# Second modulation part read from idle split buffers and partly run in the Fourier part, heads fed in pairs to the output projection

## What is computed

```python
mod_l = (silu(c) @ w_ada + b_ada).reshape(b, 6, 1, d)      # sh1, sc1, gt1, sh2, sc2, gt2
hl = rms_norm(xl, g_mix_norm) * (1 + sc1) + sh1
q, k, v, f = split(hl @ w_in)                               # k, v also for 256 context rows
attn = per head h (4), query block (2): a = softmax(q0 k0) - lam * softmax(q1 k1); o = a @ v
o = rms_norm(o, g_subln) * (1 - lambda_init)                # per head, 128 wide
fr = real(fft2(f per group)); four = fr @ w_fourier         # 4 groups of 128
xl = xl + gt1 * (concat([o, four]) @ w_out)
h2l = rms_norm(xl, g_ffn_norm) * (1 + sc2) + sh2
xl = xl + gt2 * hier_moe(h2l)                               # 32 experts, 2 a token
```

## Time and profile before

| what | us |
|---|---|
| median of 3 runs (1869.19, 1869.19, 1871.25) | 1869.19 |
| the profiled execution, its own time | 1870.13 |
| its span, first to last instruction | 1868.4 |
| PE busy in the span | 1804.5 (97%) |
| PEld (weight loads) | 1434.0 (77%) |
| DVE / ACT / POOL | 900.1 / 723.5 / 169.5 |
| mean granted clock of TensorE | 0.982 of full |

### The profile page before, as it was taken

The page is one execution under the profiler, slowest core; times in us unless marked ns, Lnnn a source line. Parts: engine busy times, 40 slices in busy tenths (PEclk is TensorE's granted clock), DMA queues, the critical chain, the costliest instruction groups (busy, mean ns, idle before and its releaser), DMA issues.

```text
span 1868.4 us, 27467 instructions
## 1 busy us (share of the span) xinstructions
PE 1804.5 (97%) x11302; PEld 1434.0 (77%) x11302; DVE 900.1 (48%) x1108; ACT 723.5 (39%) x913; POOL 169.5 (9%) x83
## 2 busy tenths in 40 slices
PE   6997899999999998999999999999999999999998
PEld 4983845545455447999987889998999899999997
DVE  4315611111111108655676575667666756566554
ACT  3424311111111116444434554455445555354443
POOL 0100000000000000111000111111111001112110
PEclk8999899999999999999899999999999999999999
DMA  9329699999999994655534265555555554455550
GB/s 336 120 91 343 228 390 422 421 422 422 422 422 422 422 406 154 208 180 185 186 129 155 69 203 181 183 199 190 188 186 192 202 181 165 159 174 182 186 195 24
DMA packets 192158, 445.65 MB, mean 239 GB/s; under 512 B 9189, under 2 KB 140638, under 8 KB 164166
## 3 DMA queue, kind: packets, MB, share of 16 engines
q1 hardware_dynamic: 188736, 437.84, 63.6%
q10 hardware_dynamic: 2918, 4.46, 0.7%
q0 software_dynamic: 416, 2.10, 0.3%
HBM read 443.31 MB, written 1.06 MB: 238 GB/s over the span
## 4 chain that ended last, share of the span: by engine, by line
PE 90%; DVE 5%; ACT 2%; DMA 1%; issue 1%; POOL 0%; ACTq 0%; DVEq 0%
PE wk L748 16%; PE wk L1158 12%; PE wk L750 8%; PE acc L720 6%; PE acc L721 6%; PE acc L722 6%; PE wk L1178 6%; PE wk L1120 3%; PE wk L720 3%; PE wk L722 3%; PE wk L721 3%; PE acc L1136 3%; PE wk L799 2%; PE wk L800 2%; PE wk L802 1%; DVE w_lo L550 1%
## 5 line engine op out<-in xcount | busy, mean ns | idle before, releaser
L550 DVE TENSOR_TENSOR w_lo<-ring,w_hi 128x2048 fp32r<-128x2048 f32 x197 | 450.5, 2289 | 237.1 <-ACT w_hi L541 236.5
L748 PE MATMUL wk<-h_both,w_hi 128*128 128x512 f32 x1344 | 476.5, 398 | 2.2 <-DVE gated L2347 1.9
L541 ACT ACTIVATE w_hi<-ring 128x2048 fp32r<-128x2048 f32 x198 | 377.4, 1907 | 244.1 <-PE acc L722 127.2
L750 PE MATMUL wk<-h_both,w_lo 128*128 128x256 f32 x1344 | 377.3, 281 | 0.0
L748 PEld LDWEIGHTS wk<-h_both,w_hi 128*128 128x128 f32 x1344 | 252.6, 188 | 64.0 <-DVE w_lo L550 2.6
L720 PE MATMUL acc<-hid_hi,w_hi 128*128 128x256 f32 x896 | 254.4, 284 | 1.4 <-DVE arena L2556 0.8
L750 PEld LDWEIGHTS wk<-h_both,w_lo 128*128 128x128 f32 x1344 | 253.9, 189 | 0.0
L721 PE MATMUL acc<-hid_lo,w_hi 128*128 128x256 f32 x896 | 253.5, 283 | 0.0
L722 PE MATMUL acc<-hid_hi,w_lo 128*128 128x256 f32 x896 | 253.4, 283 | 0.0
L1952 POOL TENSOR_TENSOR hid_lo<-gated,hid_hi 128x512 fp32r<-128x512 f32 x44 | 124.3, 2826 | 1150.7 <-ACT hid_hi L1773 1150.7
L720 PEld LDWEIGHTS acc<-hid_hi,w_hi 128*128 128x128 f32 x896 | 171.6, 191 | 4.0 <-DVE arena L2556 1.0
(11 more groups left out here) (381 smaller groups left out, 2452.7 us busy)
## 6 DMA issues: line engine op xcount, KB each, us to landing
ring<-in_ffn_w_in_dram SPq DMA_DIRECT2D x88, 1024.0 KB, 5.1
ring<-in_w_gate_dram SPq DMA_DIRECT2D x64, 1024.0 KB, 13.7
ex_ring<-in_w_up_dram SPq DMA_DIRECT2D x64, 1024.0 KB, 16.9
ring<-in_ffn_w_out_dram SPq DMA_DIRECT2D x44, 1024.0 KB, 4.9
ex_ring<-in_w_down_dram SPq DMA_DIRECT2D x32, 1024.0 KB, 13.6
arena<-in_w_down_dram SPq DMA_DIRECT2D x32, 1024.0 KB, 12.6
ring<-in_w_ada_dram SPq DMA_DIRECT2D x24, 1024.0 KB, 7.0
ring<-in_b_w_in_dram SPq DMA_DIRECT2D x24, 1024.0 KB, 5.1
```

The source lines that it names most:

```text
L541: nc.scalar.activation(w_hi[:, v % SPLIT, 0:n], ring[:, u % RING, 0:n], ACT.Copy).then_inc(w_hi_ready, 1)
L550: eng.tensor_tensor(w_lo[:, v % SPLIT, 0:n], ring[:, u % RING, 0:n], w_hi[:, v % SPLIT, 0:n].bitcast(F32), ALU.subtract).then_inc(w_lo_rea ...
L748: mm(banks[:, m, :], wh[:, k, f], h_both[:, k, :, :], start=k == 0, stop=False, skip_group_check=True)
L750: last = mm(banks[:, m, T:2 * T], wl[:, k, f], h_hi[:, k, :], start=False, stop=k == KT - 1, skip_group_check=True)
```

## The change

The eight units 4 to 9, 14 and 15 of the second modulation part no longer go through the ring. They are loaded in pairs into the idle split buffers: `ada_pair(a, q)` loads units a and a + 1 into `w_hi` and `w_lo` of buffer q. The pairs (4, 5), (6, 7), (8, 9) are issued when the input units 13, 14 and 15 have been used; (14, 15) when unit 9 has been used. The other eight keep the ring (`ADA_RING`); `place` and `prior` give the ring slot and the unit that held it before. Their semaphores are those of the expert ring, so the counts that the experts wait for are raised (`ada_landings`).

TensorE runs the first eight units amid the Fourier part, two after each of: two groups of `over_tokens`, the other two, `over_channels`, `own_matrix`. The first `mod_row` and `ada_cols` come at the head of attention. In the loop, steps 0 and 1 have two units, steps 2 to 5 one, steps 6 and 7 none; `mod_row(2)` comes in step 5 of ScalarE and `ada_cols(2)` in step 6 of TensorE. The output projection's first split comes in step 4 (high part) and step 6 (low part, between `combine(6)` and `combine(7)`), the second's high part in step 6. The heads' norm gives its high and low part by pairs of heads (`heads_scaled`, `heads_low`), and the output projection takes the pairs (k = 0, 1), then (k = 2, 3), as they come; only the last quarter of each of its first three units closes the unit.

```diff
+ADA_RING = (0, 1, 2, 3, 10, 11, 12, 13)
+def place(u):
+    if u < U_ADA2 + 4:
+        return u
+    return u - 6 if u < U_OUT else u - 8
+def prior(u):
+    p = place(u) - RING
+    return p if p < U_ADA2 + 4 else p + 6 if p < U_ADA2 + 8 else p + 8
...
         ex_in = [sem(f"ex_in{j}") for j in range(EX_RING)]
+        ada_in = [ex_in[RING + q] for q in range(SPLIT)]
+        ada_landings = {RING: 32, RING + 1: 64, RING + 2: 32}
         ex_done, pick_ready = sem("ex_done"), sem("pick_ready")
...
-            n = 16 * (u // RING + 1)
-            eng.wait_ge(weights_in[u % RING], n if i is None else i * (16 * TURN // RING) + n)
+            n = 16 * (place(u) // RING + 1)
+            eng.wait_ge(weights_in[place(u) % RING], n if i is None else i * (16 * TURN // RING) + n)
         TAIL = split_of(U_A + 2)
+        AFTER_ADA = {split_of(U_OUT): U_ADA2 + 6, split_of(U_OUT + 1): U_ADA2 + 8, split_of(U_OUT + 2): U_ADA2 + 16}
...
             if v >= SPLIT:
-                d = unit_of(v - SPLIT) + 1
+                d = AFTER_ADA.get(v, unit_of(v - SPLIT) + 1)
                 nc.scalar.wait_ge(unit_done, d if i is None else i * TURN + d)
...
-                p = u - RING
-                if p < 0:
+                if place(u) < RING:
                     return
+                p = prior(u)
                 v = split_of(p)
...
                 vacant(u, i)
-                sp.dma_start(dst, src).then_inc(weights_in[u % RING], 16)
+                sp.dma_start(dst, src).then_inc(weights_in[place(u) % RING], 16)
...
                 fetch(U_IN + a, slot_cols(U_IN + a), in_v[a])
-            for a in range(16):
-                fetch(U_ADA2 + a, ring[:, (U_ADA2 + a) % RING, :], ada_v[1 + a // KT, a % KT])
+            def ada_fetch(a):
+                fetch(U_ADA2 + a, ring[:, place(U_ADA2 + a) % RING, :], ada_v[1 + a // KT, a % KT])
+            def ada_pair(a, q):
+                for j in range(2):
+                    sp.dma_start(ex_ring[:, q + SPLIT * j, :], ada_v[1 + (a + j) // KT, (a + j) % KT]).then_inc(ada_in[q], 16)
+            for a in range(4):
+                ada_fetch(a)
+            for v in range(5, 8):
+                sp.wait_ge(unit_done, unit_of(v) + 1)
+                ada_pair(4 + 2 * (v - 5), v % SPLIT)
+            for a in range(10, 14):
+                ada_fetch(a)
+            sp.wait_ge(unit_done, U_ADA2 + 10)
+            ada_pair(14, 7 % SPLIT)
             for a in range(4):
...
-                arrived(u)
+                a = u - U_ADA2
+                if a < 0 or a in ADA_RING:
+                    arrived(u)
+                    w = ring[:, place(u) % RING, :]
+                else:
+                    q = 7 % SPLIT if a >= 14 else (5 + (a - 4) // 2) % SPLIT
+                    pe.wait_ge(ada_in[q], 64 if a >= 14 else 32)
+                    w = ex_ring[:, q + SPLIT * (a % 2), :]
                 for gr in range(ADA_GROUPS):
                     last = mm(accf[32 * gr:32 * gr + 32, bank * 512:(bank + 1) * 512], csil[:, k, :],
-                              ring[:, u % RING, gr * 512:(gr + 1) * 512], start=(k == 0), stop=(k == KT - 1),
+                              w[:, gr * 512:(gr + 1) * 512], start=(k == 0), stop=(k == KT - 1),
                               skip_group_check=True)
...
+            def ada_second(*units):
+                for a in units:
+                    ada_rows(U_ADA2 + a, a % KT, 1)
             pe.wait_ge(grp_out, 12)
-            for gr in range(4):
+            for gr in range(2):
                 group(lambda b: over_tokens(b, gr))
+            pe.wait_ge(rope_done, 2)
+            ada_second(0, 1)
+            for gr in range(2, 4):
+                group(lambda b: over_tokens(b, gr))
+            ada_second(2, 3)
             pe.wait_ge(grp_out, 16)
...
                 group(lambda b: over_channels(b, pair))
+            ada_second(4, 5)
             pe.wait_ge(grp_out, 18)
...
                 group(lambda b: own_matrix(b, pair))
+            ada_second(6, 7)
...
             scores(0)
+            scores(1)
+            ada_cols(1)
             for s in range(8):
-                if s + 1 < 8:
+                if 0 < s < 7:
                     scores(s + 1)
-                if s == 4:
-                    ada_cols(1)
-                for a in (2 * s, 2 * s + 1):
-                    ada_rows(U_ADA2 + a, a % KT, 1)
+                ada_second(*((8, 9), (10, 11), (12,), (13,), (14,), (15,), (), ())[s])
+                if s == 6:
+                    ada_cols(2)
                 turn(s)
...
                     head_squares(0)
-            ada_cols(2)
             values(3)
...
+            def mixed(a, ks, closes=False):
+                return project3(accf[:, a * 512:(a + 1) * 512], part[a], ks=ks, opens=ks[0] == 4, closes=closes)
+            part = [split(U_OUT)]
+            mixed(0, (4, 5))
+            head_squares(1)
+            project3(accf[:, 0:512], part[0], ks=(6, 7), opens=False, closes=False)
+            part.append(split(U_OUT + 1))
+            mixed(1, range(4, 8))
+            pe.wait_ge(mix_lo_ready, 2)
+            mixed(0, (0, 1))
+            mixed(1, (0, 1))
             pe.wait_ge(mod_ready, 2)
-            part = []
+            part.append(split(U_OUT + 2))
+            mixed(2, range(4, 8))
+            mixed(2, (0, 1))
+            pe.wait_ge(mix_lo_ready, 3)
             for a in range(3):
-                part.append(split(U_OUT + a))
-                project3(accf[:, a * 512:(a + 1) * 512], part[a], ks=range(4, 8), closes=False)
-                if a == 0:
-                    head_squares(1)
-            pe.wait_ge(mix_lo_ready, 2)
-            for a in range(3):
-                project3(accf[:, a * 512:(a + 1) * 512], part[a], ks=range(4), opens=False).then_inc(unit_done, 1)
+                mixed(a, (2, 3), closes=True).then_inc(unit_done, 1)
             pe.wait_ge(rt_side, 1)
...
                     for j in range(2):
-                        pe.wait_ge(ex_in[2 * s + j], at(16 * (p + 1), 16))
+                        pe.wait_ge(ex_in[2 * s + j], at(ada_landings.get(2 * s + j, 0) + 16 * (p + 1), 16))
...
             a_values(HEADS2 - 1)
-            pe.wait_ge(mix_lo_ready, 2 + HEADS2)
+            pe.wait_ge(mix_lo_ready, 3 + HEADS2)
             for a in range(4):
...
+            mod_row(1, U_ADA2 + 8, 1)
             exps(0)
...
                     exps(s + 1)
-                if s % 4 == 3:
-                    mod_row(1 + s // 4, U_ADA2 + 2 * s + 2, 1)
-                if s == 7:
-                    split_high(9)
                 turned(s)
-                if s == 6:
-                    split_high(8)
+                if s == 5:
+                    mod_row(2, U_ADA2 + 16, 1)
                 if s % 2 == 1 and s >= 3:
                     head_out(s // 2 - 1)
-                if s == 5:
+                if s == 4:
+                    split_high(8)
+                elif s == 5:
                     head_square(0)
+                elif s == 6:
+                    split_high(9)
             act.wait_ge(reldist_out, 16)
...
             head_root(1)
-            act.wait_ge(sub_done, 1)
-            A(h_hi[:, 0:4, :], mixT[:, 0:4, :], ACT.Copy).then_inc(mix_hi_ready, 1)
+            for j in range(2):
+                act.wait_ge(sub_done, j + 1)
+                A(h_hi[:, 2 * j:2 * j + 2, :], mixT[:, 2 * j:2 * j + 2, :], ACT.Copy).then_inc(mix_hi_ready, 1)
             split_high(11)
...
                 combine(s)
-            split_low(8)
-            dve.wait_ge(modcol_ps, 3)
-            modulation(16, 48)
-            V.scalar_tensor_tensor(a_ffn, mod[:, 32:40, 0], 1.0, g_ffn, ALU.add, ALU.mult).then_inc(mod_ready, 1)
+                if s == 6:
+                    split_low(8)
             split_low(9)
-            for j in range(2):
+            def heads_scaled(j):
                 dve.wait_ge(sub_std, j + 1)
...
                                                   ALU.mult, ALU.mult)
-                if j:
-                    last.then_inc(sub_done, 1)
-            dve.wait_ge(mix_hi_ready, 1)
-            V.tensor_tensor(h_lo[:, 0:4, :], mixT[:, 0:4, :], h_hi[:, 0:4, :].bitcast(F32),
-                            ALU.subtract).then_inc(mix_lo_ready, 1)
+                last.then_inc(sub_done, 1)
+            def heads_low(j):
+                own = slice(2 * j, 2 * j + 2)
+                dve.wait_ge(mix_hi_ready, j + 1)
+                V.tensor_tensor(h_lo[:, own, :], mixT[:, own, :], h_hi[:, own, :].bitcast(F32),
+                                ALU.subtract).then_inc(mix_lo_ready, 1)
+            heads_scaled(0)
+            dve.wait_ge(modcol_ps, 3)
+            modulation(16, 48)
+            V.scalar_tensor_tensor(a_ffn, mod[:, 32:40, 0], 1.0, g_ffn, ALU.add, ALU.mult).then_inc(mod_ready, 1)
+            heads_low(0)
+            heads_scaled(1)
+            heads_low(1)
             dve.wait_ge(mod_ready, 2)
```

## The result

The changed kernel took **1876.27 us** (median of 9 runs, 1875.45 to 1879.51), the kernel before 1869.34 us in the same comparison (9 runs, 1865.2 to 1872.76): ratio 1.0036, 95% interval 1.0027 to 1.0045. That is 6.9 us slower; the prediction was 1871.6 us with a range of 1865 to 1876.

A forecast was written before the change was run, and what follows sets the result against it. TensorE, busy 97% of the span, was taken to bound the kernel. Full-clock terms summed to -3.4 us; clock losses at the loop's end (+1.7) and inside it (+4.1) made +2.4, giving 1871.6 us, range 1865 to 1876.

The forecast's parts named there:

- 1, Fourier part: Fourier part: eight modulation units take 7.4 us, partly filling three waits; net +3.9, bounds +3.9 and +4.6 us.
- 2, the loads: Loads of the units moved into the Fourier part: they land before they are needed; cost 0.
- 3, steps of 4.82 us: Attention loop: units fill only part of TensorE's wait, so fewer units leave steps at 4.82 us; worth 0.
- 9, clock in the loop: Attention loop: two low-clock spells of 6.8 us from less TensorE work a step; +4.1 us, bounds 0 and +9.9.
- 4, low half ahead of `combine(7)`: End of the loop: `split_low(8)` ahead of `combine(7)` delays `turn(7)`; +1.5 us.
- 5 and 8, to the projection: `turn(7)` to the projection: 12.2 us becomes 4.6 at full clock, -7.6; idleness at the loop's end lowers the clock, +1.7.
- 6, the first three units: Projection's first three units: 20.3 us becomes 18.0 with heads in pairs; -2.2 us, bounds 0 and -2.5.
- 7, the fourth unit: Projection's fourth unit: TensorE waits for its split, which waits until the first unit closes; +1.0 us.
- The one-for-one rule: Stretch before the router (218.40): whatever it gains or loses goes through to the end one for one.
- the loop holds its clock: Loop keeps full clock, only the clock loss at the loop's end counts: -1.7 us, 1867.5; chance 0.20.
- the clock holds at the end too: Loop and its end keep full clock, router's low spell ends sooner: -3.4 us and about 2 more, 1863.8; chance 0.12.
- the slower one: Attention loop: clock low for most of steps 2 to 7; +6.3 us, 1875.5; chance 0.15.

The follow-up runs named there:

- kernel 1: Changed kernel with ScalarE's `split_high(10)`, the third projection unit's high half, moved ahead of the heads' norm: 1873.53 us, ratio 1.0026 to the kernel before.
- kernel 3: Changed kernel with `split_high(10)` early and unread matmuls in the waits of steps 2 to 7 (3, 3, 3, 3, 4, 8): 1870.93 us, ratio 1.0004.
- kernel 7: Kernel 4 with ScalarE's `split_high(10)` moved ahead of the heads' norm: 1864.02 us, ratio 0.9971 to the kernel before.
- kernel 8: Changed kernel with three units amid the Fourier part, thirteen in the loop, `split_high(10)` early, `split_low(8)` behind the last `combine`: 1862.94 us, ratio 0.9969.
- kernel 10: Changed kernel, eight units still amid the Fourier part, with `split_high(10)` early, `split_low(8)` late, three unread matmuls each in steps 2 to 6: 1866.03 us, ratio 0.9968.
- kernel 4: Changed kernel with all sixteen units back two a step in the loop, keeping the new loads and heads in pairs: 1868.12 us, ratio 0.9989.
- kernel 2: Changed kernel with matmuls nothing reads in the waits of steps 2 to 7 (3, 3, 3, 3, 4, 8): 1874.39 us, ratio 1.0024.
- kernel 5: Changed kernel with VectorE's `split_low(8)` moved behind the last `combine`: 1875.22 us, ratio 1.0032 to the kernel before.
- kernel 9: Changed kernel run again unchanged, for a second profile: 1876.98 us, ratio 1.0032 to the kernel before.
- kernel 11: Kernel 8 with `split_low(8)` and `split_high(10)` back where the changed kernel has them: 1869.81 us, ratio 1.0000 to the kernel before.
- kernel 6: Changed kernel with matmuls nothing reads in the loop's waits, only 3 in step 6 and 4 in step 7: 1871.54 us, ratio 1.0013.

## Why the prediction was wrong

The direction of most steps held, and the sum missed mostly by one step that had the wrong sign. Measured against the profiled executions, term by term:

| the prediction's step | predicted | measured | |
|---|---|---|---|
| 1, Fourier part (A) | +3.9 | +4.6 | its other bound |
| 2, the loads | 0 | 0 | right |
| 3, steps of 4.82 us | 0 | 0 | right: B is 38.23 or 38.24 us at full clock |
| 9, clock in the loop (B) | +4.1 | +4.75 | right in kind and size |
| 4, low half ahead of `combine(7)` (C) | +1.5 | +1.3 | right against before |
| 5 and 8, to the projection (D) | -7.6 and +1.7 | -4.6 | clock worth 3.0, not 1.7 |
| 6, the first three units (E) | -2.2 | +1.6 | **wrong** |
| 7, the fourth unit (F) | +1.0 | +1.1 | right |
| sum | +2.4 | +8.8 | |

*Part 6 failed*, by 3.8 of the 6.4 us that are missing. It took the first pair's scaling to stay as short as it was, 0.88 us, and asked only whether the second pair would be late. The trace of before had the warning in it: GpSimd's low half, 4.58 us long, ran from 195.11 to 199.69, beside VectorE's reciprocal, and the scaling began at 199.95, 0.26 us behind its end. Nothing in the diff moved that instruction or its releaser, ScalarE's `split_high(10)` between the squares and the root of the second heads. But part 5 brought the two pairs of heads close together: before, the first scaling (193.84) was over when GpSimd began; after, GpSimd began 0.54 us ahead of it, and the heads in pairs made this first scaling the one that the projection waits for. Kernels 1, 3, 7, 8 and 10 have the scaling at 0.88 us, the others at 4.5 to 4.7, and the difference is the place of one ScalarE instruction; it is worth 3.5 us of time (4 against 7). A part of it is clock: while TensorE stood for its 3.1 us, or within 1.5 us of its restart, a spell of low clock began in kernels 2, 4, 5, 9 and 11. E is 23.4 us in kernels 2, 5, 9 and 11, and 21.9 in the kernel after and kernel 6, which had no such spell there.

The kernel before had the hold-up itself in its trace, in the rotation. VectorE's addition of two tensors in the SBUF took 0.69 us, and 1.35 when it began beside a multiplication on GpSimd; it ended at 124.31, 0.55 behind GpSimd's end at 123.76:

```profile
121.64 0.69 DVE L2106 TENSOR_TENSOR arena<-scr 128x512 f32<-128x512 f32 x1
...
122.47 1.29 POOL L1981 TENSOR_TENSOR scr<-arena,con 128x512 f32<-128x512 f32 x1 [52.34 <-DVE arena L2106]
...
122.96 1.35 DVE L2106 TENSOR_TENSOR arena<-scr 128x512 f32<-128x512 f32 x1
```

The Trainium skill's page "SBUF — State Buffer", section "Who interferes with whom", has the mechanism: VectorE and GpSimd share one pair of ports, taken as an exclusive lock for a whole instruction. The rows agree, down to the reciprocal with its single input, which did not wait. A bound of "0 to -2.5" for part 6 left this out.

*Parts 8 and 9, the clock.* That units taken out of the waits cost clock was right, and kernel 6 shows it: the same order of work with idle time filled has B back at 38.24 and D at 4.62, exactly the "4.6 us" of part 5 at full clock. The size in B was near (4.75 against 4.1), though it isn't a fixed one: in kernels 1 and 5, whose code is the same up to the sixth step, B was 39.9, with one short spell instead of three. At the end of the loop I took half a spell of 6.8 us on idleness; it was 10.2 us long, 187.4 to 197.65, and lay on both turns, the first of the two `values` (3.62 us) and the sums (1.90 us); D lost 3.0 us by it. Part 4 is larger than it looks: with the low half out of the way (5) C falls by 2.2 us, of which against before only 1.3 shows, since there two units filled the place.

*Part 1* took the lower of its bounds; the 0.7 us of "tail" were not to be had. Kernel 8 shows what the waits hold: one unit each for 0.5 us in all. The other five cost 0.8 us apiece (4.1 in all), and in the loop they would have been free.

*The one-for-one rule* held roughly: the rest after the router's start lies between 1649.3 and 1651.9 us in all kernels but one (1647.1). It was 1651.6 to 1651.9 in the four with the router's narrow matmuls in 13.7 us of low clock, before among them, and mostly less in the others. That, with the 1.35 us ahead of A and a profiled execution high among its runs, is why 6.9 us of median stand beside 9.4 between the profiles.

Of the rivals, "the loop holds its clock" and "the clock holds at the end too" fell; the slower one was nearest, by luck: its time (1875.5) is within 0.8 us of the measured one for the wrong reason, as its price was all clock, where 3.8 of the 6.4 us were the port's.

What stays open: why the low spells in the loop are sometimes three and sometimes one in the same code, what part of kernel 8's lead over kernel 7 is real, and what eight units amid the Fourier part cost in time once the clock is held (kernels 8 and 10).

## What to carry to other kernels

Where a change takes out a wait, look at what then lies side by side: here 4.6 us of GpSimd, off the path and untouched by the diff, slid ahead of a two-input operation of VectorE and stopped the kernel for 3.5 us. Work in TensorE's waits is not only free but may hold up its clock, so fill a wait with no more than fits it, and take filler out of one place only where it doesn't have to be paid in another. Of a change with several parts, run the part that needs no trade by itself: the idle buffers and the heads in pairs were worth 5.4 us once one instruction stood elsewhere, and moving the units on top of them added next to nothing in the best version (1.1 us, within the noise) and took it all away in the given one.

## What was not expected of the hardware

The hold-up lasts for all that is left of GpSimd's instruction: the same two scalings took 0.88 us alone and 4.5 to 4.7 when GpSimd had begun 0.5 to 0.7 us ahead of them, ending 0.7 us behind it, while the one-input reciprocal beside the same instruction took 3.35 us in every profile. And matmuls without any use made a kernel faster: 19 of them (kernel 6) took 4.8 us off (4.3 by the ratios), and the useful ones ran at 2.4 GHz throughout the loop (granted clock 1.00, B 38.24 us).
